# One-core hybrid encoder layer: first group's gate stage with bank reads ahead of weight preparation, output stage with output weights as the stationary side

## The reference

```python
p = rms_norm(x, norm_g) @ w_in                     # 1024 -> 5376 columns, split into:
aq, ak, av, ag, bq, bfg, bi, bg, ma, mb = split_projection(p)
attn_o = window attention (128 keys, 8 query heads, 2 kv heads, sinks, partial rotary)
rec_o  = chunkwise gated linear recurrence, 4 heads of 128 x 128 state
ya = (attn_o * silu(ag)) @ w_ba
yb = (per-head rms norm of rec_o * g_norm * silu(bg)) @ w_bb
merged = sigmoid(ma) * ya + sigmoid(mb) * yb
y = rms_norm(x + merged @ w_o, final_g)
```

## Time and profile before

| | us |
|---|---|
| median of 3 runs (1603.17 to 1603.66) | 1603.62 |
| the profiled execution's own time | 1606.24 |
| its span, first to last instruction | 1604.2 |
| TensorE busy | 1538.0 |
| VectorE, ScalarE, GpSimd busy | 927.8, 512.9, 224.2 |
| mean granted TensorE clock | 0.985 |

### The profile page before, as it was taken

The page is one execution under the profiler, slowest core; times in us unless marked ns, Lnnn a source line. Parts: engine busy times, 40 slices in busy tenths (PEclk is TensorE's granted clock), DMA queues, the critical chain, the costliest instruction groups (busy, mean ns, idle before and its releaser), DMA issues.

```text
span 1604.2 us, 23628 instructions
## 1 busy us (share of the span) xinstructions
PE 1538.0 (96%) x9427; PEld 1433.4 (89%) x9427; DVE 927.8 (58%) x1471; ACT 512.9 (32%) x1114; POOL 224.2 (14%) x155
## 2 busy tenths in 40 slices
PE   7999999878899999999999999999999999999997
PEld 6998899778899789999999999879999999999975
DVE  5667877863367644567777136645467758414613
ACT  5355553433223222555223120212256423211002
POOL 1431224245444400000100000100000010000000
PEclk9999999988999999999999999999999999999998
DMA  4743344367787563222236885535322233886451
GB/s 154 282 158 129 125 150 160 122 237 278 265 320 271 194 242 139 106 89 102 86 108 220 273 287 201 178 130 204 127 92 101 91 109 109 260 275 213 133 189 72
DMA packets 95963, 279.94 MB, mean 175 GB/s; under 512 B 11888, under 2 KB 22896, under 8 KB 95856
## 3 DMA queue, kind: packets, MB, share of 16 engines
q1 hardware_dynamic: 70800, 204.25, 37.4%
q10 hardware_dynamic: 25056, 74.20, 11.9%
HBM read 195.57 MB, written 82.84 MB: 174 GB/s over the span
## 4 chain that ended last, share of the span: by engine, by line
PE 86%; DVE 9%; issue 2%; ACT 2%; DMA 1%; POOL 0%; ACTq 0%; DVEq 0%
PE bank L1273 22%; PE bank L1275 21%; PE bank L1274 21%; PE bank L1504 4%; PE bank L1505 4%; PE bank L1506 4%; PE bank L1475 2%; PE bank L1401 1%; PE bank L1419 1%; PE bank L1433 1%; PE bank L1471 1%; PE bank L1443 1%; PE bank L1457 1%; PE bank L1410 1%; DVE rs L1150 1%
## 5 line engine op out<-in xcount | busy, mean ns | idle before, releaser
L1273 PE MATMUL bank<-x_hi,w_unit 128*128 128x320 f32 (+2 forms) x1680 | 555.5, 331 | 34.0 <-ACT u_sum L869 27.5
L1275 PE MATMUL bank<-x_hi,w_unit 128*128 128x320 f32 (+2 forms) x1680 | 545.4, 325 | 0.0
L1274 PE MATMUL bank<-x_lo,w_unit 128*128 128x320 f32 (+2 forms) x1680 | 544.9, 324 | 0.0
L1273 PEld LDWEIGHTS bank<-x_hi,w_unit 128*128 128x128 f32 x1680 | 318.8, 190 | 45.7 <-issue 36.4
L1274 PEld LDWEIGHTS bank<-x_lo,w_unit 128*128 128x128 f32 x1680 | 319.1, 190 | 0.1
L1275 PEld LDWEIGHTS bank<-x_hi,w_unit 128*128 128x128 f32 x1680 | 318.6, 190 | 0.0
L591 POOL TENSOR_TENSOR w_unit<-w_raw,w_unit 128x512 fp32r<-128x512 f32 x102 | 142.3, 1414 | 309.2 <-ACT w_unit L646 283.3
L1504 PE MATMUL bank<-w_unit,m_hi 128*128 128x512 f32 (+1 forms) x288 | 116.2, 404 | 4.0 <-issue 3.8
L1505 PE MATMUL bank<-w_unit,m_hi 128*128 128x512 f32 (+1 forms) x288 | 113.7, 395 | 0.0
L1506 PE MATMUL bank<-w_unit,m_lo 128*128 128x512 f32 (+1 forms) x288 | 113.5, 394 | 0.0
L1255 DVE TENSOR_TENSOR res<-res,bank 128x512 f32<-128x512 f32 (+1 forms) x36 | 24.7, 685 | 114.0 <-PE bank L1506 114.0
(11 more groups left out here) (203 smaller groups left out, 2570.1 us busy)
## 6 DMA issues: line engine op xcount, KB each, us to landing
w_unit<-w_parts SPq DMA_DIRECT2D x274, 512.0 KB, 4.1
w_parts<-w_unit ACTq DMA_DIRECT2D x137, 512.0 KB, 4.0
w_raw<-in_w SPq DMA_DIRECT2D x88, 256.0 KB, 3.5
res<-in_x SPq DMA_DIRECT2D x15, 512.0 KB, 7.2
out_y<-res SPq DMA_DIRECT2D x15, 512.0 KB, 4.0
raw<-in_w SPq DMA_DIRECT2D x28, 256.0 KB, 4.3
x_raw<-in_x_t SPq DMA_DIRECT2D x12, 384.0 KB, 8.1
x_raw<-in_x_t SPq DMA_DIRECT2D x12, 320.0 KB, 5.7
```

Of the source, the lines that this page charges most:

```text
L1273: pe.matmul(out, w_h, m_h, start=first, stop=False, **more)
L1274: pe.matmul(out, w_h, m_l, start=False, stop=False, **more)
L1275: return pe.matmul(out, w_l, m_h, start=False, stop=last_of_bank, **more)
```

## The change

Two parts. **Gate stage:** the product's own reads now come ahead of the preparation where the product is an a11; elsewhere preparation stays first. In group 0 the split of the t tensors is reordered (`t_high` 1 and 2 on ScalarE ahead of two preparations; the low parts are steps of their own, `t_low`, on VectorE behind the s3 sum), product 0 comes ahead of prep 4 and 5, and SP waits one sum less before it reloads `raw_1`. **Output stage:** 8 output blocks of 128 channels, with output weights as the stationary side, through the code of the projections; 16 steps, half by half for blocks 0 to 3, then s = 0 of blocks 4 to 7, then s = 1 of them. `res` and y lie transposed (the host turns the array's axes), squares are added up on VectorE, summed over partitions by a ones matmul (`y_sum`), and `y_back` multiplies by the reciprocal root. y_sum 1 and y_back 1 of a group run in the next group's first projections. The bank rotation now starts at 2 g. The x steps are cut into smaller pieces.

```diff
+X_STEPS = {0: [("x_square", 0, 0)], 2: [("x_sum", 0, 0)], 4: [("x_square", 1, 0), ("x_split", 0, 0)],
+           5: [("x_split", 0, 1)], 8: [("x_sum", 1, 0), ("x_split", 1, 0)], 9: [("x_split", 1, 1)]}
+OUT = ([(j, s) for j in range(KT // 2) for s in range(2)] + [(j, s) for s in range(2) for j in range(KT // 2, KT)])
...
     out += [(kind, n, s) for s in range(2) for n in ("ak", "av", "bf0") for kind in ("proj", "evac")]
+    if g:
+        out[4:4] = [("y_sum", 1, g - 1)]
+        out[7:7] = [("y_back", 1, g - 1)]
...
-        out += {2 * len(firsts) - 4: prep(0, 1), 2 * len(firsts) - 2: prep(2, 3)}.get(n, [])
-        out += {1: [("t_high", 0, 0)], 2: [("t_high", 1, 0), ("t_high", 2, 0)]}.get(n, [])
-    out += [("t_last", 0, 0)] + prep(4) + [("finish", B_HEADS - 1, 0)]
-    for n in range(NO):
-        out += prep(n + AHEAD) + [("prod", n, 0)]
+        if n == 2 * len(firsts) - 4:
+            out += prep(0, 1)
+        out += {1: [("t_high", 0, 0)], 2: [("t_high", 1, 0), ("t_high", 2, 0), ("t_low", 0, 0)]}.get(n, [])
+        if n == 2 * len(firsts) - 2:
+            out += prep(2, 3) + [("t_low", 1, 0), ("t_low", 2, 0)]
+    out += [("t_last", 0, 0), ("prod", 0, 0)] + prep(4) + [("t_low", 3, 0)] + prep(5) + [("finish", B_HEADS - 1, 0)]
+    for n in range(1, NO):
+        out += ([("prod", n, 0)] + prep(n + AHEAD))[::1 if OPS[n][0] == "a11" else -1]
...
-    for p in range(KT):
+    for n, (j, s) in enumerate(OUT):
         if not last:
-            out += {0: X_STEPS[:1], 1: X_STEPS[1:2], 2: X_STEPS[2:4], 4: X_STEPS[4:]}.get(p, [])
-        out.append(("out", p // 4, p % 4))
+            out += X_STEPS.get(n, [])
+        out.append(("out", j, s))
+        if (j, s) == (KT - 3, 1):
+            out += [("y_sum", 0, g), ("y_back", 0, g)]
+    if last:
+        out += [("y_sum", 1, g), ("y_back", 1, g)]
...
-    count, use, proj = list(count), {}, 0
+    count, use, proj = list(count), {}, 2 * g
-        if s[0] in ("proj", "ya", "yb"):
+        if s[0] in ("proj", "ya", "yb", "out"):
             bs, proj = [proj % 3], proj + 1
...
-                sp.wait_ge(s_made, 4 * p)
+                sp.wait_ge(s_made, 4 * p - 1)
+                sp.wait_ge(w_split, split_count(OP["a11", p - 1]))
             sp.dma_start(raw_1[:, 0:4, :], w[b, :, 0:4, :]).then_inc(raw_in[0], 16)
...
+        def store_y(g, s):
+            lo, hi = sub(s)
+            for q in range(4):
+                k = slice(2 * q, 2 * q + 2)
+                sp.wait_ge(y_made, 8 * g + 4 * s + q + 1)
+                sp.dma_start(y[g, :, k, lo:hi], res[:, k, lo:hi]).then_inc(y_out, 16)
...
                 elif kind == "out":
-                    ahead(f"wo{a}{s}")
+                    if s == 0:
+                        ahead(f"wo{a}")
...
+                    wait_read(act, g, last, step, bank)
+                    if n >= 4:
+                        act.wait_ge(y_added, SQUARES * g + n - 3)
+                    act.activation(y_acc[:, lo:hi] if n < 2 else y_sq[:, n % 2, 0:hi - lo], res[:, a, lo:hi],
+                                   ACT.Square).then_inc(y_squared, 1)
+                    act.activation(res[:, a, lo:hi], res[:, a, lo:hi], ACT.Copy,
+                                   scale=fgain[:, a:a + 1]).then_inc(y_scaled, 1)
+                elif kind == "y_sum":
+                    act.activation(y_acc[:, lo:hi], pb[b][:, 0:hi - lo], ACT.Sqrt, scale=1.0 / D_MODEL,
+                                   bias=eps[:]).then_inc(read[b], 1)
...
+                elif kind == "out":
+                    wait_full(dve, g, last, step, bank)
+                    dve.wait_ge(res_in[a // 2], 16 * (g + 1))
+                    dve.tensor_tensor(r, r, pb[bank][:, 0:hi - lo], ALU.add).then_inc(read[bank], 1)
+                    if n > 2:
+                        add_out_squares(g, n - 1)
+                    if n == len(OUT) - 1:
+                        add_out_squares(g, n)
+                elif kind == "y_back":
+                    link(dve.reciprocal(y_acc[:, lo:hi], y_acc[:, lo:hi]))
+                    dve.wait_ge(y_scaled, len(OUT) * (s + 1) - (0 if a else KT // 2))
+                    for k in range(KT):
+                        r = res[:, k, lo:hi]
+                        ins = dve.tensor_tensor(r, r, y_acc[:, lo:hi], ALU.mult)
+                        if k % 2:
+                            ins.then_inc(y_made, 1)
...
-                if kind == "proj":
+                if kind in ("proj", "out"):
+                        mh, ml = (x_hi, x_lo) if kind == "proj" else (m_hi, m_lo)
                         ins = three_pass(pb[bank][:, 0:hi - lo], high_of(u)[:, k % 4, :], low_of(u)[:, k % 4, :],
-                                         x_hi[:, k, lo:hi], x_lo[:, k, lo:hi], k == 0, k == KT - 1)
+                                         mh[:, k, lo:hi], ml[:, k, lo:hi], k == 0, k == KT - 1)
...
+                elif kind == "y_sum":
+                    pe.matmul(pb[b][:, 0:hi - lo], ones[:], y_acc[:, lo:hi], start=True, stop=True).then_inc(full[b], 1)
```

More of the change, by code:

```diff
@@ L254, in program @@
     gate_b = own("gate_b", [P, B_HEADS, T], F32, at_gb_lo)
-    res = own("res", [P, NT, D_MODEL], F32, at_ga_hi)
+    res = own("res", [P, KT, T], F32, at_ga_lo)
     w_unit, w_raw, w_at = [], [], []
@@ L542, in body @@
                 load_block(g, b)
+                if g and b == HALVES // 2 + 1:
+                    store_y(g - 1, 1)
             if g == 0:
@@ L608, in body @@
                     x_back(t_top[:, 0], 0, 1)
-                if name == (BLOCK["wo03"], 1) and not last:
+                if name == (BLOCK["wo3"], 1) and not last:
                     add_squares(pool, 1, g + 1)
@@ L688, in prepare_x @@
             else:
-                for q in range(4):
+                for q in (2 * step[2], 2 * step[2] + 1):
                     k = slice(2 * q, 2 * q + 2)
@@ L699, in _ @@
         act.activation(root[:], eps[:], ACT.Sqrt)
-        for step in X_STEPS:
+        for step in X_ALL:
             prepare_x(step, None, 0, False)
@@ L703, in _ @@
                 high(0)
-            if step == ("x_split", 0, 0):
+            if step == ("x_split", 0, 1):
                 for b in range(1, FIRST):
@@ L917, in prepare_x @@
             elif kind == "x_split":
-                rms = x_acc[:, s, 1, 0:n]
-                wait_read(dve, g, last, ("x_sum", s, 0), 6 + s)
-                link(dve.reciprocal(rms, rms))
+                rms, part = x_acc[:, s, 1, 0:n], step[2]
+                if part == 0:
+                    wait_read(dve, g, last, ("x_sum", s, 0), 6 + s)
+                    link(dve.reciprocal(rms, rms))
                 def x_low(q):
@@ L928, in x_low @@
                                       ALU.subtract).then_inc(x_split, 1)
-                for q in range(4):
+                for q in (2 * part, 2 * part + 1):
                     for kt in (2 * q, 2 * q + 1):
@@ L956, in _ @@
         dve.wait_ge(gain_in, 16)
-        for step in X_STEPS:
+        for step in X_ALL:
             prepare_x(step, None, 0, False)
-        dve.wait_ge(consts_in, 16 * 7)
+        dve.wait_ge(consts_in, 16 * 8)
         link(dve.tensor_scalar(neg_sink[:], sink[:], -1.0, None, ALU.mult))
@@ L1248, in body @@
                     split(m_hi[:, a, lo:hi], m_lo[:, a, lo:hi], va).then_inc(merged, 1)
-                elif kind == "out" and s == 3:
-                    for i, (t0, n) in enumerate(TILES):
-                        b = OUT_BANKS[i]
-                        r = res[0:n, i, 512 * a:512 * a + 512]
-                        wait_full(dve, g, last, ("out", a, 0), b)
-                        dve.wait_ge(res_in[i], 16 * (g + 1))
-                        dve.tensor_tensor(r, r, pb[b][0:n, :], ALU.add).then_inc(read[b], 1)
-                        if a == 1:
-                            wait_read(dve, g, last, ("out", 1, 0), b)
-                            dve.sem_inc(summed, 1)
-                            if i > 1 and last:
-                                final_norm(g, i - 2)
+                elif kind == "out":
+                    n = OUT.index((a, s))
+                    lo, hi = sub(s)
+                    bank = bank_of(g, step)
+                    r = res[:, a, lo:hi]
+                    wait_full(dve, g, last, step, bank)
[6 more added lines that the diff above has]
+                elif kind == "y_back":
+                    lo, hi = sub(a)
+                    wait_read(dve, g, last, ("y_sum", a, s), 3 + a)
+                    link(dve.reciprocal(y_acc[:, lo:hi], y_acc[:, lo:hi]))
[5 more added lines that the diff above has]
+                            ins.then_inc(y_made, 1)
                 elif kind.startswith("x_"):
                     prepare_x(step, g, g + 1, last)
-            for i in range(NT - 2 if last else 0, NT):
-                final_norm(g, i)
-            dve.wait_ge(y_made, NT * (g + 1))
         groups(dve, body)
```

158 lines of the change are left out of this document (65 added, 93 removed).

## The result

The changed kernel takes 1584.99 us (median of 4 runs, 1582.11 to 1586.32) where the kernel before, beside it on the same chip, takes 1603.64 (1603.17 to 1605.47): ratio 0.988, 95% interval 0.9865 to 0.9896. It is 18.7 us faster; 28.4 were forecast.

What follows compares the result with a forecast made beforehand. TensorE, busy 96% of the span, was taken as the bound. Gate stages -20.4 and +0.75, output stages -0.9, -5.4 and -8.2, y_sum 1 +0.9 and the end +4.9 gave -28.4 from the 1603.62 median: 1575 us, range 1557 to 1591.

Steps and rivals of the forecast that it cites:

- rival A: Whole kernel: the forecast's own sum of terms holds, giving 1567 to 1583 us; chance 0.50.
- Rival C: Group 0's gate stage: the raw-buffer loop keeps about 17 us a pair; -7 instead of -20.4, 1588 us; chance 0.20.
- First gap of the gate stage: Group 0, first pair: TensorE's wait for the u_sum copy falls from 12.3 to about 5.0 us.
- Gap at the first s4: Group 0's gate stage: VectorE's finish of head 3 delays its take of s1's bank; 4.3 us of new gap.
- Period of a pair: Group 0's gate stage: seven products take 14.5 us, 17.2 before, leaving 1.0 us of gap a pair.
- Clock in that stage: Group 0's gate stage: low clock in first pairs lies inside waits for VectorE, costing little more; half a microsecond allowed.
- Gate stages of groups 1 and 2: With the bank rotation running on, group 1's a11 waits for a sigmoid, +0.75 us; group 2 nothing.
- Output stage on TensorE: 384 narrower matmuls replace 288 of 512 columns: -8.9 us a stage, -8.2 in the last group, before stalls.
- rival D: Output stages: weight loads at 190 ns each set the pace, 11 us more a group, 1609 us; chance 0.03.
- Stalls in the output stages: VectorE's x operations delay bank reads, in group 0 also wo6's cast: 8.0 us in group 0, 3.5 in group 1.
- The end: Behind the last output matmul: y_back 0, reads, sum, root, reciprocal, products and store take 16.3 us against 11.4, +4.9.
- Rival B: Whole kernel: nothing new stalls, pairs take 13.5 to 14 us, VectorE empties banks in time; -45, 1558 us; chance 0.23.

Runs made afterwards that it cites:

- gate_only: The kernel before with the gate stage's part of the change alone; 1591.13 us, ratio 0.9924.
- out_only: The changed kernel with the gate stage's part undone, so the output stage's part alone; 1596.91 us, ratio 0.9958.
- finish_late: The changed kernel with VectorE's finish of head 3 moved from before the first takes to behind the first pair's s4; 1584.17 us, ratio 0.9881.
- sum_after_takes: The changed kernel with preparation of the next pair's s3 and a22, including VectorE's s3 sum, behind the takes; 1582.25 us, ratio 0.9864.
- small_writes: The changed kernel writing and later loading the split gate weights at an eighth of their size, leaving out part of the computation; 1573.33 us, ratio 0.9808.
- casts_early: The changed kernel with ScalarE casting wo6 behind step 7 and wo7 behind step 8, ahead of their turn; 1583.03 us, ratio 0.9868.
- casts_before_copies: The changed kernel with wo6's cast behind step 7 and wo7's cast also ahead of x_split(1,0)'s copies; 1578.44 us, ratio 0.9849.
- combined2: The changed kernel with takes before s3's sum, u_sum's copy before a22's cast, group 0's product 0 before t_last, early root table, casts_before_copies' casts; 1574.78 us, 0.9822.

## Why the prediction was right, and where it was off

**What bounds the kernel** held: all of the gain came out of TensorE's gaps in group 0 and its work in the output stages, and gate_only and out_only add up.

**How near it came.** The time, 1585.0, is 10 us above the 1575 forecast. It lies above the 1567 to 1583 of rival A, my own sum, and nearer to C's 1588; it is inside the range because that took in most of C. So the change's sign and its two sources were right, and a third of the gain did not come.

**First gap of the gate stage**: 5.0 forecast, 4.26 measured. **Gap at the first s4**: 4.3 forecast, 3.21 measured, at the place named; finish_late showed that the finish is only one of two things that hold it.

**Period of a pair**: 14.5 forecast, 15.66 measured. This is the term of the stage that was mis-sized: for the five periods from the first s4 to the sixth the sum had 5 x 13.46 + 2.6 + 4.0 = 73.9 us, and they took 78.3. These 4.4 us are the stage's whole miss; the other terms came out within 0.6 us each and cancel. I priced one loop, sums, casts, subtractions and ScalarE's queue, with "the pair's last load" inside a stretch read off the pair of before. In the changed kernel VectorE stands for the load of raw_2's first half, 5.2 us, and with that wait moved out of the takes' way (sum_after_takes) the chain through ScalarE still keeps 15.24. small_writes shows the cause behind both: with 0.35 of DMA share in place of 0.75 the load takes 2.8 us and the period is 13.5. The trace of before had a hint: VectorE's L1186 waits 25.5 us in three waits for such a load there, and the one of raw_2's first half lands in 5.0 us (median), which I had not read. Rival C, that the loop over the raw buffers keeps about 17 us a pair, was right in mechanism and wrong in size: the loop gave 15.66.

**Clock in that stage**: half a microsecond forecast, 4.6 us in three stretches at 1.2 GHz measured, and 1.9 more at the edges of the waits. I wrote that low clock lies inside waits for VectorE and costs little more. The stretches themselves are not idle: they follow a wait, with TensorE busy. But their cost went where I said: 1.4 us of the first one into the gap at the first s4 (3.21 us, some 4.7 without it), the other two into the waits of the next pair, 0.15 and 0.20 us where pairs without a stretch wait about 2. This is worked out from the starts in one trace; no edit tested it.

**Gate stages of groups 1 and 2**: +0.75 forecast, +0.74 in group 1, as a wait of 0.67 for a sigmoid; nothing in group 2.

**Output stage on TensorE**: right. In group 2, without stalls, the 384 matmuls and y_sum 0 take 61.97 us (62.2 forecast), 0.160 each, though their weight loads are shown at 189 ns: rival D falls. The profile page's groups for them:

```profile
L1299 PE MATMUL bank<-m_hi,w_unit 128*128 128x384 f32 (+1 forms) x384 | 126.3, 329 | 10.2 <-POOL w_unit L610 6.4
...
L1299 PEld LDWEIGHTS bank<-m_hi,w_unit 128*128 128x128 f32 x384 | 72.6, 189 | 13.1 <-issue 6.9
```

A third of the matmuls is shown at 329 ns each and the starts are half as far apart: a shown duration is no price here. The Trainium skill's N/2.4 + 2.5 ns (TensorE: Matmul & The Clock Gate, "Back-to-back issue gap"), which that page gives for an isolated matmul, made 57.3 us of the 384 by my estimate. Group 2 took 61.97 with y_sum 0, and the measurement decides. The narrower stream won 8.4 us there.

**Stalls in the output stages**: the mechanism was right, the sizes were not. Group 1: 3.5 forecast, 1.4 measured; group 0: 8.0 forecast, and measured 6.4 for weights, 2.4 for VectorE and 1.5 of low clock, 10.3 together, with 0.2 to 0.3 more at the edge of each of the four waits. These stalls are the second term that was too small. The wait for wo6 has the cause that I named (its cast behind x_split(1,0)'s copies; casts_early removes it), its size was 4.8 and not 4.3, and the wait for wo7 and the clock behind it were not in my sum. casts_before_copies shows that VectorE's additions alone cost 6.1 us once the weights are there in time, against 3.5 forecast: the late weights hid that this part was too small as well.

**The end**: +4.9 forecast, +2.9 measured. The order was right (y_back 0 still runs, then two reads, sum, root, reciprocal, eight products, store). Too long were the steps up to the additions (+3.7 us forecast, VectorE is through with them 2.9 behind the last matmul), the eight products at their shown duration instead of their distance (4.5 forecast, 3.84 measured), and the last store (3.8, 3.4 measured). **y_sum 1 in the next groups**: 0.45 each forecast, 0.57 and 0.56 measured.

**Rival B** (no stall, 1558) fell by the gaps listed. In sum: -28.4 forecast, -22.4 in the profiles and -18.7 in the medians. Of the 6.0 us between the first two, 4.4 are group 0's gate stage, 3.6 its output stage, 1.0 the later start, -2.0 the end and -1.1 the output stage of group 1. The last 3.7 lie in no stage: they are how the two profiled executions stand to their medians, and I had taken a sum made against one of them off the median. The end and group 1's output stage came out better than forecast and hide 3.1 us of the miss, which is luck.

**Open**: why out_only's gate stage waited 1.4 us less and had 1.2 us less of low clock than before's with the same order, and why combined2's output stage had a stretch of low clock that casts_before_copies' hadn't with the same waits. In what way the writes lengthen the load (queues, DMA engines, memory) was not separated.

## What to carry to other kernels

When a wait is taken away, list every load that the waiting engine's queue still stands behind, with its landing time in that stage, before working out the new period: raw_2's 5.0 us and VectorE's 25.5 us of idle time in front of a DMA were there to be read. The idle time alone proves nothing, since small_writes has 24.4 us of it and no stall; the landing time has to be put into the loop. A busy stretch at 1.2 GHz behind a gap cost TensorE about 1.5 us here; it adds to the time only where no wait stands behind it to take it up. And when late data covers a second wait (weights before bank reads here), an edit that removes the first wins only the difference.

## What was not expected of the hardware

- A 256 KB load beside the writes of split weights landed in 5.2 us (median), with the DMA share at 0.75 and 279 GB/s over the stage; with an eighth of the written bytes, 0.35 and 104 GB/s, it landed in 2.8.
- The low clock comes behind the gap, with TensorE busy: some 3.3 us granted 0.52 after waits of 4.26, 3.21 and 2.46 us, none after waits of 2.16 and 1.63 in the same stage, and none in casts_before_copies' output stage with four waits up to 1.94, after the last of which combined2 has one.
- VectorE's products of 384 columns start 0.48 us apart, those of 320 0.41; a single addition of 384 columns is shown as 0.54.
